# Memory products and grid bias moved into the expert stage, and a rewritten routing chain

## The reference, cut to what matters

```python
# first block, after its mixers: routing (one expert group of four, two experts of its eight)
lg = (xs @ wr_g) + br_g;  ptop, gsel = lax.top_k(softmax(lg), 1)
le = ((xs @ wr_e) + br_e).reshape(-1, MOE_GROUPS, MOE_PER_GROUP)   # of the group gsel
lv, esel = lax.top_k(le, MOE_TOPK);  we = softmax(lv) * ptop
# second block, in each of its layers l = 0, 1
mk, mv = split(rms_norm(mem, norm_mem_g) @ w_mem_kv, 2)      # mem: 256 x 1024, an input
mo = memory_attention(rms_norm(mq), rms_norm(mk), mv)        # norms by head of 64
bias = rpb[:, row_off + 7, col_off + 15]                     # na_rpb: 4 x 15 x 31 by layer, an input
sc = q . k * d ** -0.5 + where(col_mask, bias, NEG_INF)
```

## Time and profile before

| what | value |
|---|---|
| runs | 2827.93 / 2832.22 / 2834.94 us |
| the profiled execution's own time | 2831.34 us |
| its span | 2829.7 us, 31050 instructions |
| PE busy | 2644.2 us (93%) |
| DVE, ACT, POOL busy | 1082.7, 786.4, 887.7 us |
| DMA | 344.15 MB, mean 122 GB/s |
| mean granted clock of PE | 0.962 of full |

### The profile page before, as it was taken

The page is one execution under the profiler, slowest core; times in us unless marked ns, Lnnn a source line. Parts: engine busy times, 40 slices in busy tenths (PEclk is TensorE's granted clock), DMA queues, the critical chain, the costliest instruction groups (busy, mean ns, idle before and its releaser), DMA issues. The chain is left out here.

```text
span 2829.7 us, 31050 instructions
## 1 busy us (share of the span) xinstructions
PE 2644.2 (93%) x12444; PEld 1929.7 (68%) x12444; DVE 1082.7 (38%) x1832; ACT 786.4 (28%) x1123; POOL 887.7 (31%) x273
## 2 busy tenths in 40 slices
PE   7989788999879997898999999999998999999998
PEld 5854446867643332685788888888684888888887
DVE  1156535457231113466444411112367344411111
ACT  1022322133111112525422332222425322422221
POOL 4710000013113332231344443444240344444443
PEclk9989889989969998999999999999999999999999
DMA  4423111034458994222122222232321222222223
GB/s 162 149 82 123 42 49 41 1 134 134 178 200 356 391 388 185 92 94 73 63 101 99 95 90 104 90 104 91 123 104 45 90 90 104 90 93 101 93 100 119
DMA packets 84870, 344.15 MB, mean 122 GB/s; under 512 B 34446, under 2 KB 34830, under 8 KB 49144
## 3 DMA queue, kind: packets, MB, share of 16 engines
q1 hardware_dynamic: 63640, 314.39, 30.4%
q10 hardware_dynamic: 7264, 19.35, 2.1%
q0 software_dynamic: 13824, 8.44, 1.0%
HBM read 385.19 MB, written 28.21 MB: 146 GB/s over the span
## 5 line engine op out<-in xcount | busy, mean ns | idle before, releaser
L161 POOL TENSOR_TENSOR w_lo<-w_raw,w_hi 128x2048 fp32r<-128x2048 f32 x149 | 692.7, 4649 | 1614.6 <-ACT w_hi L154 1567.6
L185 PE MATMUL bank<-xh,w_hi 128*128 128x512 f32 x1704 | 671.8, 394 | 32.9 <-DVE xl L350 19.5
L186 PE MATMUL bank<-xl,w_hi 128*128 128x512 f32 x1704 | 666.3, 391 | 0.0
L187 PE MATMUL bank<-xh,w_lo 128*128 128x512 f32 x1704 | 666.2, 391 | 0.0
L185 PEld LDWEIGHTS bank<-xh,w_hi 128*128 128x128 f32 x1704 | 321.9, 189 | 118.2 <-issue 23.1
L154 ACT ACTIVATE w_hi<-w_raw 128x2048 fp32r<-128x2048 f32 x152 | 290.8, 1913 | 368.5 <-PE bank L185 336.5
L187 PEld LDWEIGHTS bank<-xh,w_lo 128*128 128x128 f32 x1704 | 321.7, 189 | 67.8
L186 PEld LDWEIGHTS bank<-xl,w_hi 128*128 128x128 f32 x1704 | 322.0, 189 | 67.3 <-issue 1.2
L185 PE MATMUL bank<-ha,w_hi 128*128 128x512 f32 x480 | 186.7, 389 | 0.0
L186 PE MATMUL bank<-hb,w_hi 128*128 128x512 f32 x480 | 186.7, 389 | 0.0
L187 PE MATMUL bank<-ha,w_lo 128*128 128x512 f32 x480 | 186.7, 389 | 0.0
(11 more groups left out here) (579 smaller groups left out, 3648.0 us busy)
## 6 DMA issues: line engine op xcount, KB each, us to landing
w_raw<-weights SPq DMA_DIRECT2D x193, 1024.0 KB, 4.8
ring<-weights SPq DMA_DIRECT2D x45, 1024.0 KB, 14.5
before_halves<-weights SPq DMA_DIRECT2D x18, 1024.0 KB, 14.4
res<-weights SPq DMA_DIRECT2D x16, 1024.0 KB, 11.7
early_gates<-gate_rows SPq DMA_DIRECT2D x20, 256.0 KB, 2.0
ahead<-early_gates ACTq DMA_DIRECT2D x20, 256.0 KB, 2.7
res<-xT ACTq DMA_DIRECT2D x2, 2048.0 KB, 9.1
distance_bias<-distance_bias_once ACTq DMA_DIRECT2D x8, 512.0 KB
```

Of the source, the lines that this page charges most:

```text
L161: engine.tensor_tensor(self.lo[:, s, :], self.raw[:, s, :], self.hi[:, s, :].bitcast(F32), ALU.subtract).then_inc(self.split, 1)
L185: self.released(pe.matmul(out, hi, moving[0], start=start, stop=False))
L186: pe.matmul(out, hi, moving[1], start=False, stop=False)
L187: return pe.matmul(out, lo, moving[0], start=False, stop=stop)
```

## The change

The memory rows are squared, summed and scaled for both layers beside `project` and stored in DRAM. Keys and values of both layers are plain f32 products in the expert stage: five groups of eight between the last pass and the tail, three groups inside the tail. The grid bias of both layers is made in eight products of 32 rows beside the routing chain. `prepare` loads finished keys and values; the key norm becomes a seventh job beside the six head norms, rotations stand one tile later, and the pool products stand inside the second token-major block. In the routing the router is the stationary operand, ACT adds the bias and PE turns the 36 rows of logits back to tokens; the ranks take five products in place of fourteen; one pair of DVE operations stands ahead of its wait; the clearing of the gather rows moves from DVE to POOL, and one activation table that holds both ln and exp is loaded ahead of the norm.

```diff
 def project(...):
-            ws.load(sp)
+            ws.load(sp, upto=6)
+            if "loads" in memory_run:
+                memory_run["loads"](sp, *memory_sems)
...
+                if j == tiles // 2 + 6 and "tensor" in memory_run:
+                    memory_run["tensor"](pe, *memory_sems)
...
+def memory_rows(k, mem, scaled, gains, total):
...
+    def scalar(...):
+        act.activation(scaled, mem, ACT.Square).then_inc(mem_squared, 1)
+        act.activation(total, k.bank[4][:, 0:256], ACT.Ln, scale=1.0 / D, bias=k.eps[:, 1:2]).then_inc(mem_log, 1)
+        act.activation(total, total, ACT.Exp, scale=-0.5).then_inc(mem_rstd_ready, 1)
+        for t in range(KT):
+            act.activation(scaled[:, t, :], mem[:, t, :], ACT.Copy, scale=gains[:, 0, t:t + 1]).then_inc(mem_scaled0, 1)
...
+    def tensor(...):
+        pe.matmul(k.bank[4][:, 0:256], const(k, "ones"), total, start=True, stop=True).then_inc(mem_summed, 1)
...
+    def vector(...):
+        dve.tensor_reduce(total, scaled.rearrange("p t n -> p n t"), AX.X, ALU.add).then_inc(mem_reduced, 1)
...
+    def vector_end(...):
+        dve.tensor_tensor(mem, mem, every, ALU.mult).then_inc(mem_normed, 1)
...
 def moe(...):
...
+            for i in range(LAYERS):
+                for n, src in zip(mem_numbers[i], (k.mem_dram[i, :, :, :].rearrange("p t n -> p (t n)"),
+                                                   ws.dram[MEM_FIRST + MEM_CHUNKS * i, :, :],
+                                                   ws.dram[MEM_FIRST + MEM_CHUNKS * i + 1, :, :])):
+                    wait_used(sp, n - RING)
+                    sp.dma_start(slots[n % RING], src).then_inc(mem_in[i], 16)
...
+            for i in range(LAYERS):
+                sp.wait_ge(mem_copied, 2 * i + 2)
+                sp.dma_start(k.kv_dram[i, :, :], mem_out[i]).then_inc(mem_stored, 16)
...
-                for q in range(4):
-                    last = pe.matmul(k.bank[4 + q][:, 0:36], k.res[:, t, tile(q)], router[:, t, :], start=t == 0,
-                                     stop=t == KT - 1)
+                last = pe.matmul(k.bank[4][0:36, :], router[:, t, :], k.res[:, t, :], start=t == 0, stop=t == KT - 1)
             last.then_inc(logits_ready, 1)
+            pe.wait_ge(logits_copied, 1)
+            for q in range(4):
+                last = pe.transpose(k.bank[5][:, 36 * q:36 * q + 36], logit_rows[:, tile(q)], ident[0:36, 0:36])
+            last.then_inc(logits_turned, 1)
...
+            for r in range(4):
+                out = k.bank[0][:, 32 * r + 32:160].rearrange("p (a e) -> p a e", e=32)
+                pe.matmul(out, ones, mask[:, r:r + 1, :].to_broadcast([128, 4 - r, 32]), start=r == 0, stop=False, skip_group_check=True)
+            last = pe.matmul(k.bank[0][:, 0:128], up, every, start=False, stop=True, skip_group_check=True)
...
+            pe.wait_ge(grid_in, 32)
+            pe.wait_ge(rows_out, 8)
+            for u, c in enumerate(grid_order):
+                rows = slice(32 * (c // 2), 32 * (c // 2) + 32)
+                if u >= 5:
+                    pe.wait_ge(grid_copied, u - 4)
+                pe.matmul(grid_bank[u][0:n_grid, :], tab[rows, :], select_rows[rows, SEQ * (c % 2):SEQ * (c % 2) + SEQ],
+                          start=True, stop=True).then_inc(grid_ready, 1)
...
+            pe.wait_ge(turned_copied, PASSES)
+            pe.wait_ge(mem_in[0], 48)
+            for p in range(2):
+                memory_keys(0, p)
+            for q in range(2):
+                memory_values(0, q)
+            pe.wait_ge(mem_in[1], 48)
+            memory_keys(1, 0)
+            behind = [lambda: memory_keys(1, 1), lambda: memory_values(1, 0), lambda: memory_values(1, 1)]
...
+                if q == 1:
+                    pe.wait_ge(res_ready2, 1)
+                if q < 3:
+                    behind[q]()
...
+            act.preload_act_table_set("natural_log_exp_and_others")
             norm["scalar"](act, *norm_sems)
+            act.wait_ge(logits_ready, 1)
+            act.activation(logit_rows, k.bank[4][0:36, :], ACT.Identity, bias=route_bias).then_inc(logits_copied, 1)
...
+            for u, c in enumerate(grid_order):
+                act.wait_ge(grid_ready, len(grid_order) if u == 7 else u + 1)
+                act.activation(grid_rows[u][0:n_grid, :], grid_bank[u][0:n_grid, :], ACT.Copy).then_inc(grid_copied, 1)
+                act.wait_ge(grid_copied, u + 1)
+                act.dma_start(k.grid_dram[:, SEQ * c:SEQ * c + SEQ], grid_rows[u][0:n_grid, :]).then_inc(grid_stored, 16)
+            act.wait_ge(grid_stored, 16 * len(grid_order))
             rows_low(0)
...
+            memory_out(0)
+            memory_out(1)
             for q in range(4):
+                if q == 2:
+                    memory_out(2)
...
-            for q in range(4):
-                step(dve.tensor_tensor(lg[:, q, :], k.bank[4 + q][:, 0:36], route_bias, ALU.add))
+            dve.wait_ge(logits_turned, 1)
+            step(dve.tensor_copy(lg[:, :, :], k.bank[5][:, 0:144].rearrange("p (q e) -> p q e", e=36)))
...
+            of_pick(numbers[:, 0:32], ex)
             dve.wait_ge(ranks_ready, 1)
...
 def prepare(...):
+    heads.append((mk[:, :, :].rearrange("p a n -> p (a n)"), par("memk")))
...
-                    if 2 <= j < 10:
-                        bias_rows(j - 2)
...
+                        if m and t == 6:
+                            pe.wait_ge(mats_in, 16)
+                            pe.wait_ge(rows_copied, 1)
+                            for p in range(2):
+                                pe.wait_ge(pool_ready, p + 1)
+                                pe.matmul(k.bank[4 + p][:, :], k.mats2[:, 128 * p:128 * p + 128], sums[:, p, 0:SEQ],
+                                          start=True, stop=True).then_inc(pool_product, 1)
```

More of the change, by code:

```diff
@@ L74 @@
 T2_TILES = 14
+NA_TABLE = 60
 class Kernel:
@@ L352, in split_start, with project @@
     return names, dict(scalar=scalar, gpsimd=gpsimd, tensor=tensor, vector=vector)
-def project(k, tiles, out, token_major, moving=None, n_moving=SEQ, first=None, aside=None):
+def project(k, tiles, out, token_major, moving=None, n_moving=SEQ, first=None, aside=None, memory_aside=None):
     ws = k.ws
@@ L376, in _ @@
                 aside_run["loads"](sp, *aside_sems)
-            ws.load(sp)
+            ws.load(sp, upto=6)
+            if "loads" in memory_run:
+                memory_run["loads"](sp, *memory_sems)
+            for c in range(6, ws.to_load):
+                sp.wait_ge(ws.split, ws.turn + (c - SLOTS + 1))
+                sp.dma_start(ws.raw[:, c % SLOTS, :], ws.dram[ws.turn + (ws.skipped + c), :, :]).then_inc(
+                    ws.loaded[c % SLOTS], 16)
+            if "loads_end" in memory_run:
+                memory_run["loads_end"](sp, *memory_sems)
             if "sync_end" in first_run:
@@ L421, in _ @@
                     aside_run["vector"](dve, *aside_sems)
+                if j == tiles // 2 + 4 and "vector" in memory_run:
+                    memory_run["vector"](dve, *memory_sems)
+                if j == tiles // 2 + 8 and "vector_end" in memory_run:
+                    memory_run["vector_end"](dve, *memory_sems)
             for m, (rows, width) in enumerate(token_major):
@@ L2266, in prepare @@
     cos, sin, turned = (k.yb[:, j, :] for j in (4, 5, 6))
[L2267 to L2270 removed]
+    rotate, blk = const(k, "rotate"), const(k, "blk64")
     n_pad = SEQ + 16
@@ L2411, in _ @@
                 ws.round(act, chunk0 + 1)
-                act.wait_ge(mem_in, 16)
-                act.activation(work[:, :], region[:, 0:2048], ACT.Square).then_inc(mem_squared, 1)
                 for j in range(T2_TILES):
@@ L2961, in build @@
         for i in range(LAYERS):
-            layer(k, i, grid_dram, k.dram["outT"] if i == LAYERS - 1 else None)
+            layer(k, i, k.dram["outT"] if i == LAYERS - 1 else None)
             assert k.ws.blocks == 16 * (c0 + (i + 1) * LAYER_CHUNKS)
@@ L3030, in weight_stream @@
     for l in range(LAYERS):
+        parts += [fm_blocks(v["w_mem_kv_2"][l][:, 0:256]), tm_blocks(v["w_mem_kv_2"][l][:, 256:512])]
+    for l in range(LAYERS):
         w2 = v["w_in_2"][l]
```

350 lines of the change are left out of this document (164 added, 186 removed).

## The result

After the change the runs take 2782.43 us in the median (2777.07 to 2783.41, 4 runs), against 2833.58 (2827.93 to 2835.61, 4 runs) for the kernel before beside them: a ratio of 0.9816, with a 95% interval from 0.9803 to 0.983. The prediction said 2782 (2771 to 2797). The profiled execution took 2783.41 us, its span is 2781.6, against 2831.34 and 2829.7 before. So 48.1 us went, of the 50.0 forecast. The close number is partly luck, as the table shows. The table divides both spans at the same events; its last column is the forecast.

A forecast was written before the change was run, and what follows sets the result against it. PE was taken to bound nearly the whole span, with a serial chain in the routing. Prepare -43.2, project +0.6, routing -9.2 and tail +1.8 gave -50.0 from 2831.34: 2781.3, as median 2782 us, range 2771 to 2797.

The forecast's parts named there:

- Prepare: Prepare stage, both layers: removed PE work counts in full, 21.6 us less a layer, 43.2 in both; bounds 36 to 45.
- Grid products: Prepare: eight grid-row products leave, each holding PE 0.99 us, 7.9 us a layer.
- The end: End of prepare, last token-major product to next stage's first: of 19.15 us 5.6 stay, so 13.5 go.
- The cover of 0.7 us: Prepare: DVE needs 30.3 us ahead of the pool products, PE 31.0, so DVE's work stays hidden by 0.7 us.
- (a): Routing, norm: the second table load, between ln and exp, goes, -1.3 us.
- (b): Routing, router products: 4.3 us behind the last tile for 7.5, -3.2 (-4.5 to +1.6), half the products at low clock.
- (c): Routing, ranks: ten records for 28 at 0.21 us each, set by weight load, not columns, -3.8 us.
- (d): Routing: one pair of DVE operations over 256 elements moves into DVE's wait, -0.9 us.
- (e): Routing, grid products between ranks and places: 0 to +4.8 us, taken as 0 because different row groups work in parallel.
- Rival 4: Routing: grid stores, if one after another, hold the experts back, slower than before from 9 us a store; chance 0.02.
- Expert tail: Behind the last expert pass: forty memory products free in PE's wait, three groups inside push the last turn; +1.8 us (-1 to +6).
- Beside project: Memory sums beside project: one 256-column product against the ones and a restart add 0.6 us, 1.3 if it waits.

The follow-up runs named there:

- experiment 6: Changed kernel with eight 32-row products of 512 columns, read by nothing, put back into prepare in both layers: 2792.75 us, one run.
- experiment 9: Changed kernel with the clearing of the pool's 1,056 columns on DVE in prepare done four times instead of once: 2778.86 us, one run.
- experiment 4: Changed kernel without the table preload ahead of the norm, so ACT loads a table ahead of ln and another before exp: 2782.85 us, one run.
- experiment 5: Changed kernel with the eight grid products in order 0 to 7, so neighbours use the same 32 rows of PE: 2780.87 us, one run.
- experiment 1: Changed kernel with the four routing cuts undone (router products, ranks, second table load, DVE pair), router bias left out: 2792.35 us, 4 runs.
- experiment 10: Changed kernel with 512-column products that nothing reads filling three waits of PE in the routing: 2783.78 us, one run.
- experiment 7: Changed kernel with all eight groups of memory products ahead of the expert tail's first turn, none between turns: 2790.64 us, one run.
- experiment 11: Changed kernel with one unread 512-column product behind the last product of attention in both layers: 2781.58 us, one run.
- experiment 8: The kernel before the change, run once more unedited for its trace: 2830.32 us.

## Why the prediction was right, point by point

- **Prepare** (forecast -21.6 a layer, measured -23.5 and -22.3). Grid products: -8.5 for -7.9 (experiment 6). The step counted 0.99 from one row to the next, but each also costs the weight products behind it a restart, 1.21 in all; a new wait of 0.8 takes some back. The end: 19.15 less 3.37 and 1.96 is -13.8 for -13.5. The head sum adds 0.87 (6.32 less 5.45) for 1.0. These and the memory sum's 1.2 make -22.6; the rest is not assigned. Together the two layers gave 45.8, just outside the prediction's own bounds of 36 to 45, mostly through the grid products. The cover of 0.7 us was 1.1, and experiment 9 used it up.
- **Routing** (-9.2, measured -11.3). (a) -1.1 for -1.3. (b) The mis-sized term: -4.4 for -3.2. The forecast took half of the wide products at the low clock, because the earlier trace rows shows 0.50 there; that was the clock of the narrow stream, and the wide one ran at 1.00. It did so in all nine traces in which PE had paused 3.3 us ahead of it. After the 4.7 us of experiment 4 it was at 0.50 for 3.4 us and then at 1.00 again. So the preload of (a) had a part in (b), a link that the prediction doesn't make. (c) -4.3 for -3.8, again the clock: 0.12 a record where 0.21 was assumed. Its reason, that a record's columns don't count, stands; that the weight load sets its time was argued and not tested. (d) -0.9 as forecast. (e) 0 as forecast, and for the reason that the prediction took from the Trainium skill, "TensorEngine Tiling (Array Packing)", Key Properties: the clock was at 0.50 and the products overlapped (experiment 5). The place products gave nothing back. Of the other 0.6 us, 0.4 lies between the place products and the first turned rows and 0.2 between the logits and the mask.
- **Stores of the grid.** The cover was given as 10 us with a landing of 2.5. The landing goes by the traffic: 2.4 to 2.6 us in experiment 1, where the queues had drained, 6.8 to 9.6 in experiment 9, 6.9 to 11.3 in experiment 10. The changed kernel's trace has no landings of these stores. In experiments 5, 6, 7, 9 and 11, whose routing is timed like its own, the last store lands 1.9 to 2.5 us before ACT copies the first turned rows, in experiment 10 1.5 us. Nothing was lost, but by a margin of some 2 us and not of ten. Rival 4 had the right place; its assumption that stores go one after the other is not what happened: in experiment 10 eight stores issued 1.0 us apart, each taking 6.9 to 11.3 us, were all in within 18.3 us of the first issue.
- **Expert tail** (+1.8, measured +0.8). First turn 20.99 us from the last pass' start, 20.96 before. The last turn is 2.7 later for 3.3; the sums behind it gave back 2.1 for 1.5, and 0.2 lies between them and the next stage.
- **Beside project** (+0.6): head norm's first table load stands at 165.8 to 166.9 in the changed kernels that have it, at 165.4 and 166.0 in the two traces of before, so about +0.8 on average.
- **Not forecast.** Some 3.7 us around mixer C and 1.5 at each feed-forward stretch, all in untouched code. The mean granted clock is 0.54 over head norm and 0.72 over the 6 us ahead of the first feed-forward stretch's table load, where before had 0.99 and 1.00 (experiment 8). That the sum hit is luck: this loss and the larger gains, neither of them forecast, nearly cancel.

## What to carry to other kernels

A clock read beside one form of an instruction is no forecast for another form: a stream of short records and one of 512 columns, after the same pause of 3.3 us, got different clocks in the same place. Nor is it one for another pause: the wide stream began low when the pause was 4.7 us. A chain that is shortened moves into other traffic; look at the DMA share at its new position, since a landing time is that of the queue it was read in (2.6 or 11.3 us for the same store). And when a change gives tens of us, unchanged stretches may move by several: compare by stage before crediting an edit.

## What was not expected of the hardware

- Eight f32 products of 32 rows by 512 columns, on four groups of rows, took 6.8 us at a granted clock of 0.50, half of the estimate for one after another; 8.2 with neighbours on the same rows. At 1.00 they took 5.0 (experiment 10), not half of 6.8, since the last ones wait for ACT's copies of 1.0 us each.
- A pause of PE is followed by the low clock in one execution and not in the next: the same code up to there, a mean of 0.54 over 16 us in the changed kernel and of 0.90 in experiment 4. PE with no pause over 0.5 us held 1.00 where it fell otherwise (experiment 10, 792 to 811 us).
- One DVE operation beside each of POOL's subtractions of 4.6 to 4.8 us at the end of prepare takes 4.1 to 5.6 us, for 0.4 to 1.3 otherwise, whichever stands there (the changed kernel and experiment 9).
- A gather of rows needs 4.2 to 4.5 us when the last weights have landed as it is issued, and 6.7 when the DMA engines stay full for 3.2 us more (experiment 10).
